# Expert stage of a two-layer diffusion step: expert 3's gate and up weights issued ahead of the scattered rows, the first further rows loaded by GpSimd, 18 instead of 26 constant products between the layers

## The reference

```python
scores = sigmoid(xt @ w_router)                      # 16 experts in 4 groups
best group by its two best scores, then the top 2 experts inside it
w = chosen scores / their sum
act = silu(einsum('nd,edf->nef', xt, w_gate)) * einsum('nd,edf->nef', xt, w_up)
y = einsum('nef,efd->nd', act * gates, w_down)       # D_FF = 512
x = x + g2 * y
```

## Time and profile before

| | us |
|---|---|
| median of three runs | 1472.4 |
| lowest, highest | 1472.06, 1473.91 |
| the profiled execution's own time | 1473.27 |
| its span (first to last instruction) | 1471.3 |
| TensorE busy in the span | 1327.3 (90%) |
| VectorE busy | 476.2 (32%) |
| ScalarE busy | 328.4 (22%) |
| GpSimd busy | 256.9 (17%) |
| first layer's expert stage, first to last expert product | 474.7 to 732.0 |
| second layer's expert stage | 1187.6 to 1444.5 |

### The profile page before, as it was taken

One profiled execution on the slowest core, in us unless ns is written; L12 is line 12 of the kernel. 1 busy time (PEld: TensorE's weight loads), 2 busy tenths in 40 slices (PEclk: granted clock), 3 DMA queues, 4 the chain that ended last, 5 costly groups with the idle time before them and its releaser, 6 DMA issues.

```text
span 1471.3 us, 17933 instructions
## 1 busy us (share of the span) xinstructions
PE 1327.3 (90%) x7009; PEld 746.0 (51%) x7010; DVE 476.2 (32%) x855; ACT 328.4 (22%) x505; POOL 256.9 (17%) x225
## 2 busy tenths in 40 slices
PE   6999999999999977689899999999999988997772
PEld 2655446675545443345446554555654554553341
DVE  2424326762144101111144352576413521110003
ACT  2136416631001000000021662464100110000001
POOL 2620017721001000000037000683100010000001
PEclk9999999999999999999999999999999999999996
DMA  9781426553829899999973221466412589999994
GB/s 346 257 295 66 172 86 218 212 186 143 281 102 380 336 396 396 396 395 390 361 252 125 94 82 57 173 230 228 158 58 114 224 348 379 405 389 391 399 412 178
DMA packets 105726, 371.90 MB, mean 253 GB/s; under 512 B 7376, under 2 KB 22064, under 8 KB 89280
## 3 DMA queue, kind: packets, MB, share of 16 engines
q1 hardware_dynamic: 84816, 327.33, 58.6%
q0 software_dynamic: 6928, 23.98, 4.5%
q10 hardware_dynamic: 13920, 19.74, 3.9%
HBM read 341.60 MB, written 29.43 MB: 252 GB/s over the span
## 4 chain that ended last, share of the span: by engine, by line
PE 75%; DMA 17%; DVE 4%; ACT 1%; issue 1%; SPq 1%; ACTq 0%; POOL 0%; DVEq 0%; POOLq 0%
PE pG L1587 25%; PE pG L1579 10%; DMA ring<-in_w_exp_down_dram 9%; PE pS L1676 8%; PE pG L1828 6%; PE pG L1692 5%; DMA hT_gen<-in_w_exp_up_dram 3%; DMA ring<-in_w_exp_up_dram 3%; PE pG L1540 3%; PE pX L1507 2%; PE pX L1676 2%; DMA ring<-in_w_mod_dram 2%; PE pX L1656 2%; PE pS L1656 2%; PE pS L1601 2%; PE pX L1642 1%
## 5 line engine op out<-in xcount | busy, mean ns | idle before, releaser
L1587 PE MATMUL pG<-hT_gen,ring 128*128 128x384 f32 x1024 | 339.6, 489 | 1.6 <-ACT hT_gen L955 1.6
L1587 PEld LDWEIGHTS pG<-hT_gen,ring 128*128 128x128 f32 x1024 | 191.8, 190 | 134.5 <-issue 6.6
L1676 PE MATMUL pS<-ring,hT_gen 128*64 128x256 f32 x1408 | 160.1, 383 | 27.6 <-DMA ring<-in_w_exp_up_dram 15.2
L1579 PE MATMUL pG<-ring,hT_gen 128*128 128x512 f32 (+1 forms) x384 | 148.7, 543 | 1.8 <-DVE hT_gen L1112 1.6
L1676 PEld LDWEIGHTS pS<-ring,hT_gen 128*64 128x64 f32 x1408 | 101.8, 138 | 91.9 <-DMA ring<-in_w_exp_up_dram 19.7
L1467 DVE TENSOR_TENSOR hT_gen<-pS,hT_gen 128x256 f32<-128x256 f32 x32 | 19.3, 602 | 371.2 <-PE pS L1676 371.2
L1579 PEld LDWEIGHTS pG<-ring,hT_gen 128*128 128x128 f32 x384 | 71.5, 190 | 70.0 <-issue 64.3
L741 POOL DMA_INDIRECT hT_gen<-y_scr,idx x12 | 11.4, 950 | 515.3 <-ACTq L1020 512.2
L1692 PE MATMUL pG<-ring,hT_gen 128*64 128x512 f32 x352 | 82.1, 608 | 18.6 <-issue 8.2
L982 ACT COPY hT_gen<-pG 128x512 f32<-128x512 f32 x32 | 18.8, 586 | 300.2 <-PE pG L1692 300.2
L1828 PE MATMUL pG<-ring 128*128 128x512 f32 x192 | 83.3, 593 | 2.5 <-DVE ring L1351 2.5
(11 more groups left out here) (282 smaller groups left out, 1643.9 us busy)
## 6 DMA issues: line engine op xcount, KB each, us to landing
ring<-in_w_mod_dram SPq DMA_DIRECT2D x24, 2048.0 KB, 8.2
ring<-in_w_exp_up_dram SPq DMA_DIRECT2D x22, 2048.0 KB, 33.6
ring<-in_w_exp_down_dram SPq DMA_DIRECT2D x22, 2048.0 KB, 34.9
ring<-in_w_exp_gate_dram SPq DMA_DIRECT2D x22, 2048.0 KB, 27.6
ring<-in_w_in_dram SPq DMA_DIRECT2D x20, 2048.0 KB, 7.9
modb<-in_w_exp_gate_dram SPq DMA_DIRECT2D x10, 2048.0 KB, 34.2
hT_gen<-in_w_exp_up_dram SPq DMA_DIRECT2D x10, 2048.0 KB
rows_nw<-in_w_exp_down_dram SPq DMA_DIRECT2D x10, 2048.0 KB, 38.2
```

The lines of the kernel that those rows point to most:

```text
L1579: ins = pe.matmul(ps[:, 0:width], hT[:, k, t * P:(t + 1) * P], w[:, k, 0:width], start=(k == 0), stop=(k == KC - 1))
L1587: ins = pe.matmul(ps[:, 0:TOK], w[:, k, c0:c0 + P], src[:, k, :], start=(k == 0), stop=(k == nk - 1))
L1676: ins = pe.matmul(dst[64 * hf:64 * hf + 64, 0:256], x[:, k, :], w[:, k, 256 * hf:256 * (hf + 1)], start=(k == 0), stop=(k == KC - 1))
```

## The change

Three edits, in both layers where a layer has the code.

1. SyncE's wait for `x_put` and the row loads move behind expert 3's gate and up weights. SyncE now waits for `e_gate` of expert 0, issues expert 3's gate, waits for `e_up`, issues its up, and only then waits for `x_put`, loads the rows of experts 2, 3 and 4 (six DMAs), issues expert 2's down, and waits for `e_down` before expert 3's down.
2. The two loads of the first further block move from SyncE to GpSimd, behind the scatter, with the waits for `x_put` and `y_all`.
3. `idle_products(26, 2)` becomes `idle_products(18, 2)`.

```diff
                 sp.wait_ge(route_ready, L + 1)
                 sp.wait_ge(e_gather, 2 * (L + 1))
-                sp.wait_ge(x_put, 16 * 2 * NT * (L + 1))
-                if L > 0:
-                    sp.wait_ge(y_all, L)
-                    sp.wait_ge(e_xTp, NLOAD * L)
-                for row, dst, s in ((NE, xrow_o, xo_first), *((e, xrow[e % 3], x_got[e % 3]) for e in (2, 3, 4))):
-                    for hf in range(2):
-                        sp.dma_start(dst[BLK * hf:BLK * (hf + 1), :],
-                                     x_scr[row * BLK:(row + 1) * BLK, 512 * hf:512 * (hf + 1)]).then_inc(s, 16)
-                expert(L, 2, 6, 2)
...
-                behind(0, 0)
+                sp.wait_ge(e_gate, L * NE + 1)
+                further_done(0, gate_and_up=True)
+                expert(L, 3, 0, 0)
+                sp.wait_ge(e_up, L * NE + 1)
+                expert(L, 3, 0, 1)
+                sp.wait_ge(x_put, 16 * 2 * NT * (L + 1))
+                if L > 0:
+                    sp.wait_ge(e_xTp, NLOAD * L)
+                for e in (2, 3, 4):
+                    for hf in range(2):
+                        sp.dma_start(xrow[e % 3][BLK * hf:BLK * (hf + 1), :],
+                                     x_scr[e * BLK:(e + 1) * BLK, 512 * hf:512 * (hf + 1)]).then_inc(x_got[e % 3], 16)
+                expert(L, 2, 6, 2)
+                sp.wait_ge(e_down, L * NE + 1)
+                sp.wait_ge(v_pe, sp.snap(ov) * 4 + V0)
+                expert(L, 3, 0, 2)
...
+                pool.wait_ge(x_put, 16 * 2 * NT * (L + 1))
+                if L > 0:
+                    pool.wait_ge(y_all, L)
+                for hf in range(2):
+                    pool.dma_start(xrow_o[BLK * hf:BLK * (hf + 1), :],
+                                   x_scr[NE * BLK:(NE + 1) * BLK, 512 * hf:512 * (hf + 1)]).then_inc(xo_first, 16)
...
-                    idle_products(26, 2)
+                    idle_products(18, 2)
```

## The result

| | before | changed |
|---|---|---|
| median of six runs, side by side (us) | 1472.93 (1471.92 to 1475.96) | 1479.01 (1475.14 to 1480.14) |
| ratio, with its 95% interval | | 1.003 [1.0016, 1.0045] |
| the profiled execution's own time | 1473.27 | 1480.08 |
| its span | 1471.3 | 1478.1 |

Slower by 0.3%, where I had said 1468.0 us, faster by 0.3%, with 1463.6 to 1471.3 for 8 in 10. The result lies outside the range and on the other side.

What follows compares the result with a forecast made beforehand. It took the DMA weight stream to bound the first layer from expert 4 on, TensorE the second until 1247.65 us; -4.7 + 1.7 - 1.4 = -4.4 us gave 1468.0 us, with 1463.6 to 1471.3 for 8 in 10.

Steps and rivals of the forecast that it cites:

- the 4.7 of the sum: First layer's expert stage: expert 3's gate and up fill unused DMA time from 484 to 497 us, -4.7 us.
- the 4.2 us: Second layer: DMA time won at 1197 but not kept, the hole moving ahead of expert 5's gate; 0 us.
- The rows behind 4 MB: Second layer, expert 1: TensorE waits 2.0 us for expert 2's rows queued behind expert 3's weights; +1.7 us after -0.3.
- the term for the hole: First layer, 484 to 497 us: unused DMA share, counting the 1 MB of rows at half rate; -4.7 us.
- rival 4: Hole worth little: only 3 us in the first layer, or a clock fall in the second's wait (+1.7); 1469.7 us, 20%.
- The bound: Upper bound on the second layer's wait for expert 2's rows, from ScalarE's same-size loads under a full stream: 8 us.
- rival 5: Rows take the 15.5 us of ScalarE's slowest load, expert 1 waits 8 us in the second layer; 1474.0 us, 3%.
- GpSimd's loads: First further block's two row loads, moved to GpSimd, arrive in time: 0 us, bound 1.5.
- Eight products fewer: Between the layers: turns start 2.9 us sooner, a clock fall costs 1.5 (bounds 0 and 3.4); -1.4 us.
- In the first layer it costs nothing: First layer: the same 2 us wait for rows falls where TensorE later idles for weights, so 0 us.

Runs made afterwards that it cites:

- e5: New order in the first layer only, with GpSimd's two loads and 26 constant products, against the kernel before: ratio 0.9966.
- e8: Only expert 3's gate ahead of the rows, its up behind them, in both layers, against the kernel before: ratio 0.9968.
- e1: The changed kernel with its 26 constant products back (new order and GpSimd's two loads stay), against the kernel before: 1476.93 us, ratio 1.0014.
- e6: New order in the second layer only, with GpSimd's two loads and 26 constant products, against the kernel before: ratio 1.0039.
- e7: SyncE waits for the scatter first, then issues expert 3's gate and up, then the rows, both layers, against the kernel before: ratio 1.0057.
- e4: The kernel before with only the first further block's two loads moved to GpSimd: ratio 0.9990.
- e2: The kernel before with 18 constant products instead of 26 and nothing else: ratio 1.0000.
- f2: Expert 3's gate alone ahead of the rows in both layers, 22 constant products, against the kernel before: 1468.35 us, ratio 0.9962.
- f1: Expert 3's gate alone ahead of the rows in the first layer, old order in the second, 22 constant products, against the kernel before: 1467.51 us, ratio 0.9949.

## Why the prediction was wrong, point by point

*The order holds.* What bounds each layer was read rightly. The first stage gained 4.0 us for the 4.7 of the sum, e5 -0.34% (5.1 us). In the second stage the same hole was closed for nothing: with the gate ahead and no wait (e8) it took 274.2 us, as e5 did with the old order, for 273.2 before. So the 4.2 us were not kept, and for the reason given: in e8 the hole stands ahead of expert 5's gate and the gate is issued at 60.05.

*The step that failed: "The rows behind 4 MB".* The sum has the weights through at 1207.8 and the first pair of rows there 1.5 us later, "less than the 2.6 us that such a load takes at least", so a wait of 2.0 us. Measured in the second stage: 6.75 (changed kernel), 6.1 (e1), 6.3 (e6), 9.5 (e7, where the rows were issued 2.5 us later than in e6). Three things were missing. In e6, where the scatter was not held up, they are these.

First, the weights' end. In e6, with the scatter as early as before, the weights were through near 1209 and not 1207.8, and the rows' own stretch followed:

```profile
1210.00:1214.00 4.00, 0.36 (x2) 0.36 (x3) 0.00 (x0) 0.00 (x0) 0.00 (x0) 0.57 1.04 242
1202.00:1206.00 4.00, 4.00 (x40) 2.66 (x38) 0.00 (x0) 0.38 (x1) 0.00 (x0) 1.00 1.01 321
```

From 1202 to 1206 GpSimd's two row loads were among the weights at 321 GB/s, where weights alone run at 399. On their own queue they took turns with the weights (packets of q0 and q1 in this stretch: 73 and 72) instead of standing behind them, and took about 4 x (1 - 321/399) = 0.8 us of the stream (an estimate from these rows). I had priced only their own landing.

Second, the rows' own time. Six loads together have the engines full at 242 GB/s, and the first pair was there at 1213.0, some 4 us after the weights had ended, not 1.5. Six loads of 131 KB at 242 GB/s are 3.2 us; the term for the hole has the rows at half rate, and this step left that out.

Third, the clock. I had a fall "during the new wait in the second layer" as part of rival 4, at 1.7 us and outside the sum. It came in all eight stages with a wait of 6 us or more. So the term is 6.3 + 2.0 = 8.3 us (the changed kernel's wait of 6.75 less the 0.42 of before, and the longer product) and not 2.0 - 0.3.

The bound stood there: "8 us: ScalarE's loads of the same size under a full stream take 12.5 in the median". Measured for SyncE's own loads: 12.1 to 14.8 in the first stage, 12.7 to 15.3 in e6. I took the value that I could construct over the one that rows of the same size under the same load showed, and gave the rival built on it (5) 3%, at 1474.0 us. It is the one that came in size: a wait of 6.3 us, and with the boundary's 1.9 us and the clock's 2.0 on top of its 1474.0 one is at 1477.9, 1.1 below the median. That this comes out so near is in part luck, since rival 5 has 8 us of waiting and 4.7 us of gain, for 6.3 and 4.0.

*The scatter's end* was taken as given. That the new loads could hold it up, by up to 10 us, is in none of my steps and none of my rivals. I had taken the stream that ends near 484.6 and 1197.3 for loads issued earlier, behind which the weights would stand; in the seven to eight microseconds before that it is the scatter's own data, and the weights run beside it. In the profiled execution it was this way, and not the order behind 4 MB, by which the rows of the second stage came late; both ways end within 0.5 us of each other (waits of 6.75 and 6.25), so it cost nothing on top.

*GpSimd's loads*: e4 fits the 0, but in the new order they took 0.8 us of the stream, as said above.

*Eight products fewer*: the gain of 2.9 and the gap of 4.0 us were right (TensorE free at 746.8, rows at 750.5). The fall of the clock was priced at 1.5, the cost of one fall inside a stage; measured -2.9 became +0.5, so it cost 3.4, the upper bound; in e2 the stretch was 0.5 us shorter than before, a cost of 2.4. Behind a gap of 3.71 us, with one more of 1.64 behind it, the clock stayed low for 11 us here, 7 in e2. The whole term, -1.4 in the sum, is 0.00% in e2 [-0.14, +0.13], which does not exclude it.

*"In the first layer it costs nothing"*, for the rows' wait, is not shown at 2 us: the one first stage with such a wait (f2, 2.18 us) took 253.3 us, for 251.6 and 251.2 without (e8, f1), less than differs by chance. At 6 to 8 us the stage is 2.3 us longer than e8's (254.0 and 253.9 against 251.6), which is little above that.

## What to carry to other kernels

A small load that an engine waits for is priced by what stands ahead of it, in bytes and on every queue, and not by its own time: here 3 us alone, 7 behind 2 MB, 14 behind 4 MB. Find out too what fills the engines ahead of the hole: here it was the scatter whose end the next step waits for, and what was moved forward ran beside it. So fill a hole with as much as the hole holds (here one load of 2 MB and not two), and check the wait where the stream is *not* the bound, since there it costs in full and takes the clock down with it. When a row of the trace shows a load of the same size under the same stream, that row is the price.

## What I had not expected of the hardware

A scatter on GpSimd's queue is held up by weight loads on SyncE's queue that are issued while its last instruction runs, or up to 1.6 us behind its end: 10.0 to 11.2 us to land with one such load of 2 MB, 15.8 with two, 5.9 to 6.5 with none near. The two queues took turns by packets and not by bytes (130 to 125), so the 4 KB packets got a fifth of what moved. And the clock stays low well beyond an idle stretch: with waits of 6.2 and 6.8 us it was at or near 0.50 for 7 and 10 us, most of it over products, and with the gap of 3.7 us between the layers for 11 us.
